# Prompt attention of a hybrid decoder layer: pairs of blocks in alternation, output copied out of PSUM at once, half the copies of the turned weights on VectorE

## The chip, the cores and the metric

The kernel runs on 1 core of one Trainium2 chip. The metric is the device time of one execution in microseconds. A core has TensorE (PE; PEld is its weight load), VectorE (DVE), ScalarE (ACT), GpSimd (POOL) and SyncE (SP), which here starts most of the transfers. The engines run side by side and wait for each other by semaphores only.

## The reference

One inference step of a layer on 1024 prompt tokens and 8 sequences of 4 new tokens, all in float32. Around the attention stand a half-step feed-forward network, a combined input projection, a convolution branch with a LayerNorm and swish, an output mix, and a second feed-forward network. What the change touches is attention over the prompt's selected keys, and the LayerNorm of the convolution branch:

```
s = index_scores(qi, ki, wi); keep the 256 best admissible keys of each query
logits = q . k * HEAD_DIM ** -0.5, NEG where a key is not kept
p = softmax(logits);  out = p @ v            # 8 heads of 64, 8 blocks of 128 queries
y = silu(layernorm(conv(u)));  A = y @ w_conv_out;  B = out @ w_attn_o
h = h + g2 * W_out(sigmoid(gate_A) * A + sigmoid(gate_B) * B)
```

## The kernel before

The prompt's queries are taken in 8 blocks of 128. Block b admits 128 (b + 1) keys, so block 7 has eight times the work of block 0. The selection has left a mask of 0 or NEG in `pick` for each block. Attention is dense over the admitted keys with that mask added. Its loop runs over NQ = 64 heads n in the order of the blocks, block 0 first (b = n // 8), and each engine has its own unrolled copy of the loop, written out in the order in which it is to work:

- TensorE (function `m2_pe`) works in units u of two heads. Iteration u holds the logits of unit u + 1 (L1524, four PSUM banks of `main`, two per head, single), the transposes of the exponentials of head 2u (`turn_weights`, L1541; keys 0 to 511 into bank 4 as part 0, the others into bank 5 as part 1), the values of unit u - 1 (L1552, into bank b % 2 of `aux`, where all 8 heads of a block collect), and the transposes of head 2u + 1. Once in a block the reciprocal sums are turned as well (`turn_sums`, L1563, bank 4).
- VectorE (`m2_dve`) adds the mask and takes the maximum of each head in one operation out of PSUM into `lb` or `lb_raw` (L1785), and makes the bias from it (L1790). For each block it later takes the reciprocal of the sums and spreads it over `otok` (L1803, L1807), multiplies the block's output in PSUM by it (L1813), and makes the low part `o_lo` (L1819).
- ScalarE (`m2_act`) takes the exponential with the sum (L1718, two heads behind VectorE), copies the turned weights of both parts out of PSUM (L1692, `pt` or `pt_n`), copies the turned sums (L1712), and makes the high part `o_hi` (L1724).

The logits of the next unit wait until VectorE has read both heads of the present one (`at_l`). Part 0 of each head waits until ScalarE's last copy has freed bank 4. There is one `otok` for all blocks, so one block's output is finished before the next one's is begun.

In the same loop, at heads 36, 39 and 42 (LN_AT), VectorE does a reciprocal (L1795) and a product (L1798) of the LayerNorm for each third of the tokens; at head 46 ScalarE does its swish (L1699), after which GpSimd splits it into high and low parts (L1394, L1396). The loop's end releases the mix: the first product L244 waits for `mix_free`, which VectorE raises after the last block's L1813, and the attention half of it waits for all of `o_lo`. SyncE loads gates and weights for it after the last transposes (`gate_load`, L1381).

## Time and profile before

| | us |
|---|---|
| median of 3 runs (lowest, highest) | 2939.66 (2937.61, 2944.67) |
| the profiled execution | 2934.1 |
| its span | 2932.3 |
| TensorE busy | 2714.8 (93%) |
| VectorE busy | 1485.8 (51%) |
| GpSimd busy | 925.3 (32%) |
| ScalarE busy | 639.0 (22%) |

Times within the profile are us from the start of the span. A group's line gives the engine, the source line, the operation and its tiles (written <- read) with their shapes. The granted clock is the share of 2.4 GHz that TensorE was allowed: 1.00 is 2.4 GHz, 0.50 is 1.2 GHz. Idle time of an engine that is not the last one costs nothing.

### The profile page before, as it was taken

To read this page: it belongs to the slowest core of one execution; us is meant where nothing else is said; L and a number is where in the kernel's file an instruction comes from. 1 tells how busy PE (TensorE), PEld (TensorE's weight loads), DVE (VectorE), ACT (ScalarE), POOL (GpSimd) and SP (SyncE) were. 2 spreads that over 40 slices of the span, in tenths; PEclk is the share of its full clock that TensorE was granted. 3 is DMA by queue.
4 is the path that set the end of the run, shared out by engine and by line. 5 is a ranking of instruction groups with operands and counts; after the bars stand their busy time and mean duration, and the time that the engine had idled before them with its cause. 6 is when DMAs were issued, how large, how long until landed. Compare 5 with 4: busy or idle time off the path is not lost.

```text
span 2932.3 us, 43345 instructions
## 1 busy us (share of the span) xinstructions
PE 2714.8 (93%) x16036; PEld 2444.0 (83%) x16036; DVE 1485.8 (51%) x2536; ACT 639.0 (22%) x1110; POOL 925.3 (32%) x490
## 2 busy tenths in 40 slices
PE   7999999999998879999998488888989999999998
PEld 3799999999997748788798235588879999999998
DVE  2434444444444548999999846454243333333333
ACT  1411111111111421123344226710041000000113
POOL 0322222222222206634698200122213323233223
PEclk9999999999999889999999689999989999999999
DMA  6322222121222313311122510044101111111111
GB/s 237 120 68 72 72 72 71 65 71 65 72 72 95 88 30 103 89 59 37 58 96 78 207 51 1 1 132 145 44 22 44 49 44 43 50 43 50 43 43 60
DMA packets 207593, 209.68 MB, mean 72 GB/s; under 512 B 13087, under 2 KB 160659, under 8 KB 206601
## 3 DMA queue, kind: packets, MB, share of 16 engines
q1 hardware_dynamic: 197324, 181.56, 19.7%
q10 hardware_dynamic: 10181, 26.90, 2.8%
q8 instruction: 60, 0.98, 0.1%
q14 instruction: 28, 0.23, 0.0%
HBM read 172.89 MB, written 28.94 MB: 69 GB/s over the span
## 4 chain that ended last, share of the span: by engine, by line
PE 68%; DVE 22%; issue 5%; ACT 3%; DVEq 1%; DMA 1%; POOL 0%; SPq 0%; ACTq 0%; POOLq 0%
PE main L244 19%; PE main L246 19%; PE main L245 19%; DVE top L1139 6%; DVE pick L1152 5%; DVE conv_y L1206 3%; PE main L333 1%; DVE pick L1126 1%; PE main L1524 1%; PE main L1541 1%; PE aux L1552 1%; ACT tmp L446 1%; PE aux L414 1%; PE aux L344 1%; PE aux L343 1%
## 5 line engine op out<-in xcount | busy, mean ns | idle before, releaser
L244 PE MATMUL main<-nhi,whi 128*128 128x352 f32 (+1 forms) x3288 | 1077.2, 328 | 28.4 <-DVE nlo L491 16.7
L246 PE MATMUL main<-nhi,wlo 128*128 128x352 f32 (+1 forms) x3288 | 1064.0, 324 | 0.0
L245 PE MATMUL main<-nlo,whi 128*128 128x352 f32 (+1 forms) x3288 | 1064.0, 324 | 0.0
L233 POOL CAST whi<-raw 128x1024 fp32r<-128x1024 f32 x189 | 203.3, 1076 | 1669.2 <-PE main L246 1279.0
L244 PEld LDWEIGHTS main<-nhi,whi 128*128 128x128 f32 (+1 forms) x3288 | 622.8, 189 | 55.9 <-issue 25.3
L245 PEld LDWEIGHTS main<-nlo,whi 128*128 128x128 f32 (+1 forms) x3288 | 624.6, 190 | 1.1
L246 PEld LDWEIGHTS main<-nhi,wlo 128*128 128x128 f32 (+1 forms) x3288 | 622.9, 189 | 1.0
L235 POOL TENSOR_TENSOR wlo<-raw,whi 128x1024 fp32r<-128x1024 f32 x189 | 475.7, 2517 | 15.2
L638 DVE TENSOR_TENSOR tmp<-main,tmp 128x352 f32<-128x352 f32 x132 | 69.2, 525 | 779.8 <-PE main L246 775.6
L657 DVE SCALAR_TENSOR_TENSOR h<-main,ada,h 128x352 f32<-128x352 f32 (+1 forms) x528 | 294.3, 567 | 97.4 <-PE main L246 97.2
L244 PE MATMUL main<-hid_hi,whi 128*128 128x352 f32 x1056 | 342.1, 324 | 0.3
L245 PE MATMUL main<-hid_lo,whi 128*128 128x352 f32 x1056 | 338.6, 321 | 0.0
L246 PE MATMUL main<-hid_hi,wlo 128*128 128x352 f32 x1056 | 338.5, 321 | 0.0
L627 ACT ACTIVATE hid_hi<-tmp 128x352 fp32r<-128x352 f32 x132 | 65.8, 498 | 637.9 <-DVE tmp L638 637.9
L244 PEld LDWEIGHTS main<-hid_hi,whi 128*128 128x128 f32 x1056 | 198.1, 188 | 5.0 <-DVE h L657 3.5
L245 PEld LDWEIGHTS main<-hid_lo,whi 128*128 128x128 f32 x1056 | 198.4, 188 | 0.5
L246 PEld LDWEIGHTS main<-hid_hi,wlo 128*128 128x128 f32 x1056 | 198.0, 188 | 0.0
L625 ACT ACTIVATE tmp<-main 128x352 f32<-128x352 f32 x132 | 60.5, 458 | 550.9 <-PE main L246 550.9
L1139 DVE MAX8 top<-pick 128x8 f32<-128x384 f32 (+5 forms) x192 | 171.4, 893 | 16.5 <-DVEq L1131 0.4
L1152 DVE MATCH_REPLACE8 pick<-top,pick 128x384 f32<-128x384 f32 (+5 forms) x192 | 168.2, 876 | 0.4 <-issue 0.3
L641 DVE TENSOR_TENSOR hid_lo<-tmp,hid_hi 128x352 fp32r<-128x352 f32 x132 | 69.3, 525 | 74.5 <-ACT hid_hi L627 74.5
L1206 DVE SCALAR_TENSOR_TENSOR conv_y<-uext,taps,conv_y 128x1024 f32<-128x1024 f32 x60 | 91.2, 1520 | 11.3 <-DVE conv_y L1206 10.9
(251 smaller groups left out, 2592.3 us busy)
## 6 DMA issues: line engine op xcount, KB each, us to landing
ada_raw<-in_w_ada SPq DMA_DIRECT2D x18, 2048.0 KB, 8.5
raw<-in_w_gate SPq DMA_DIRECT2D x44, 512.0 KB, 3.9
raw<-in_w_up SPq DMA_DIRECT2D x44, 512.0 KB, 3.8
raw<-in_w_down SPq DMA_DIRECT2D x44, 512.0 KB, 3.5
raw<-in_w_in SPq DMA_DIRECT2D x40, 512.0 KB, 3.9
gate_d<-zraw ACTq DMA_DIRECT2D x16, 528.0 KB, 2.8
gates<-gate_d SPq DMA_DIRECT2D x16, 528.0 KB, 4.7
zsw<-zraw ACTq DMA_DIRECT2D x50, 132.0 KB, 2.4
```

The costliest lines, as they stand in the source:

```text
L233: pool.tensor_copy(whi[:, slot], raw[:, slot]).then_inc(hi_done, 1)
L235: pool.tensor_tensor(wlo[:, slot], raw[:, slot], whi[:, slot].bitcast(F32), ALU.subtract)\
L244: pe.matmul(bank, whi[:, slot, w], hi(c), start=(i == 0), stop=False)
L245: pe.matmul(bank, whi[:, slot, w], lo(c), start=False, stop=False)
L246: last = pe.matmul(bank, wlo[:, slot, w], hi(c), start=False, stop=(i == n - 1))
L627: act.activation(hid_hi[:, sub, tcs(t)], tmp[:, 3 + t, :], ACT.Copy).then_inc(f["hid_hi"], 1)
L638: dve.tensor_tensor(tmp[:, 3 + t, :], main[:, 3 + t, 0:TC], tmp[:, t, :], ALU.mult)\
L641: dve.tensor_tensor(hid_lo[:, sub, tcs(t)], tmp[:, 3 + t, :], hid_hi[:, sub, tcs(t)].bitcast(F32), ALU.subtract)\
L657: dve.scalar_tensor_tensor(h[:, c, t * TC:t * TC + n], main[:, d % NBANK, 0:n], gate[:, c, 0:1], h[:, c, t * TC:t * TC + n], ALU.mult, ALU ...
L1139: dve.max(top8[0:n, :], scores).then_inc(tk, 1)
L1152: dve.match_replace(scores, top8[:, :], scores, TAKEN).then_inc(tk, 1)
L1206: dve.scalar_tensor_tensor(y, uext[:, c, bass.ds(k, SEQ)], taps[:, c, bass.ds(k, 1)], y, ALU.mult, ALU.add).then_inc(cv, 1)
```

## The change

The units come in the order of GROUPS: blocks 7 and 0 alternate, one unit (two heads) of each, then 6 and 1, 5 and 2, 4 and 3. A group has 16 heads. HEADS[n] gives block and head of the n-th head, DONE the order in which blocks end (7, 0, 6, 1, 5, 2, 4, 3), and e is a block's place in it. The finishing steps of a group's first block follow at heads end_of(e) + 0, 2, 6, 8, those of its second at + 2, 10, 14, 16, where end_of(e) = 16 (e // 2 + 1).

```diff
+        o_f = place("o_f", [P, 4, TOK], F32, HB + 16896)
-        sums = place("sums", [P, 2, H], F32, UB + 44384)
-        rinv = place("rinv", [P, 2, H], F32, UB + 44448)
+        sums = place("sums", [P, 4, H], F32, UB + 44384)
+        rinv = place("rinv", [P, 4, H], F32, UB + 45920)
...
+        GROUPS = ((7, 0), (6, 1), (5, 2), (4, 3))
+        UNITS = [(b, hp) for g in GROUPS for hp in range(H // 2) for b in g]
+        HEADS = [(b, 2 * hp + s) for b, hp in UNITS for s in range(2)]
+        PARTS = [(n, p) for n in range(NQ) for p in range(1 + (HEADS[n][0] >= 4))]
+        DONE = [b for g in GROUPS for b in g]
+        def end_of(e):
+            return 2 * H * (e // 2 + 1)
+        def same_bank(b):
+            return max([e + 1 for e in range(DONE.index(b)) if DONE[e] % 2 == b % 2], default=0)
...
 m2_pool, m == 3:
+                    for t in range(NTC):
+                        pool.wait_ge(ln_sem["rs"], t + 1)
+                        y = conv_y[:, :, tcs(t)]
+                        pool.tensor_tensor(y, y, rstd_c[t][:, :].unsqueeze(1).to_broadcast([P, 4, TC]), ALU.mult)\
+                            .then_inc(ln_sem["ml"], 1)
...
 m2_pe, turn_weights(n, turned_sums):
+                    pe.wait_ge(pt_e[part], parts_before(i, part))
+                    if part == 0:
+                        pe.wait_ge(o_c, turned_sums)
 m2_pe, values(u):
-                pe.wait_ge(pt_e, LAST_PART[2 * u + 1])
-                if hp == 0 and b >= 2:
-                    pe.wait_ge(at_m, b - 1)
+                pe.wait_ge(pt_e[0], 2 * u + 2)
+                if b >= 4:
+                    pe.wait_ge(pt_e[1], parts_before(LAST_PART[2 * u + 1], 1))
+                if hp == 0:
+                    pe.wait_ge(o_u, same_bank(b))
 m2_pe, the loop:
+                for e in range(NSEQ):
+                    if 2 * u == end_of(e) + 2 + 8 * (e % 2):
+                        turn_sums(e, min(2 * u + 1, NQ - 1))
+                        turned_sums = e + 1
...
 m2_act, turned(n), part 0 only:
+                act.activation(pt_of(n)[:, 0:k1, :], main[:, 4, 0:P * k1].rearrange("p (k n) -> p k n", n=P), ACT.Copy)\
+                    .then_inc(pt_e[0], 1)
...
 m2_dve, turned(n), part 1, called after the softmax of head n + 2:
+                dve.wait_ge(pt_t, i + 1)
+                dve.tensor_copy(pt_of(n)[:, 4:k1, :], main[:, 5, 0:P * (k1 - 4)].rearrange("p (k n) -> p k n", n=P))\
+                    .then_inc(pt_e[1], 1)
 m2_dve, the loop, for each e with b = DONE[e] and at = end_of(e) + 8 * (e % 2):
+                    if n == end_of(e) + 2 * (e % 2):
+                        dve.wait_ge(pv_mm, LAST[b] + 1)
+                        dve.tensor_copy(o_f[:, :, bass.ts(b, P)], aux[:, b % 2, :].rearrange("p (c n) -> p c n", c=4))\
+                            .then_inc(o_u, 1)
+                    if n == at + 2:      # reciprocal and spread, as before
...
+                    if n == at + 6:
+                        dve.wait_ge(o_c, e + 1)
+                        dve.wait_ge(o_u, e + 1)
+                        dve.tensor_tensor(otok[:, :].rearrange("p (c n) -> p c n", c=4), o_f[:, :, bass.ts(b, P)],
+                                          otok[:, :].rearrange("p (c n) -> p c n", c=4), ALU.mult).then_inc(at_m, 1)
+                        if e == NSEQ - 1:
+                            dve.drain().then_inc(mix_free, 3)
+                    if n == at + 8:      # o_lo, as before
```

The output's copy `o_f` lies in the place of `o_hi`. TensorE turns the sums of block e in the iteration of heads end_of(e) + 2 (+ 8), ScalarE copies them at + 5 (+ 8) and makes `o_hi` at + 7 (+ 8).

## Rows read from the trace of the kernel before

**Rows 1.** The page, busy time, share of the span and instructions by engine.
```profile
PE 2714.8 (93%) x16036; PEld 2444.0 (83%) x16036; DVE 1485.8 (51%) x2536; ACT 639.0 (22%) x1110; POOL 925.3 (32%) x490
```

**Rows 2.** By stretch: length; PE, PEld, DVE, ACT, POOL busy; granted clock; DMA.
```profile
1844.09:1876.51 32.42, 23.50 (x195) 16.67 (x195) 11.59 (x28) 25.75 (x50) 13.99 (x6) 0.84 0.00 1
...
1748.85:1910.09 161.24, 132.93 (x1088) 87.07 (x1088) 81.91 (x229) 111.46 (x255) 13.99 (x6) 0.89 0.03 8
...
1750.35:1770.90 20.55, 18.51 (x82) 9.63 (x82) 7.80 (x44) 12.03 (x44) 0.00 (x0) 0.50 0.00 0
...
1849.70:1859.60 9.90, 5.71 (x38) 4.75 (x38) 1.85 (x4) 7.79 (x16) 9.74 (x5) 0.50 0.01 2
```

**Rows 3.** Chain of waits, blocks 3, 4, 7: start, us, what.
```profile
1787.20 1.18 PE main L1524 x4
...
1790.48 1.13 PE main L1524 x4
...
1802.33 1.35 PE main L1524 x8
...
1806.10 1.40 PE main L1524 x8
...
1887.65 1.92 PE main L1524 x8
1889.57 1.02 PE main L1541 x8
1890.59 1.90 PE aux L1552 x32
...
1895.03 1.92 PE main L1524 x8
```

**Rows 4.** Timeline, two softmax heads of block 7 on VectorE.
```profile
1889.60 1.23 DVE L1785 CUSTOM_DVE_ANT_0 lb<-main,pick 128x1024 f32<-128x1024 f32 x1 [2.33 <-PE main L1524]
...
1891.01 1.22 DVE L1785 CUSTOM_DVE_ANT_0 lb<-main,pick 128x1024 f32<-128x1024 f32 x1
```

**Rows 5.** Groups by shape, attention: count, busy us, mean ns, idle before.
```profile
L1692 ACT ACTIVATE pt<-main 128x512 f32<-128x512 f32 x24 | 13.9, 596 | 11.5 <-PE main L1541 11.4
...
L1785 DVE CUSTOM_DVE_ANT_0 lb<-main,pick 128x896 f32<-128x896 f32 x4 | 4.4, 1088 | 3.9 <-PE main L1524 3.9
...
L1718 ACT ACTIVATE lb<-lb,nb 128x896 f32<-128x896 f32 x4 | 4.2, 1042 | 0.0
```

**Rows 6.** Groups by shape, VectorE, 10 to 140 us: copies out of PSUM.
```profile
L323 DVE COPY h<-main 128x512 f32<-128x512 f32 x16 | 10.0, 682 | 3.8 <-PE main L297 3.8
...
L323 DVE COPY h<-main 128x128 f32<-128x128 f32 x2 | 0.5, 277 | 0.0
```

**Rows 7.** Groups by shape, attention: operations of the LayerNorm.
```profile
L1396 POOL TENSOR_TENSOR conv_lo<-conv_y,conv_hi 128x1408 fp32r<-128x1408 f32 x3 | 9.5, 3162 | 0.2
...
L1795 DVE RECIPROCAL rstd_c<-rstd_c 128x352 f32<-128x352 f32 x3 | 7.0, 2342 | 0.0
...
L1798 DVE TENSOR_TENSOR conv_y<-conv_y,rstd_c 128x1408 f32<-128x1408 f32 x3 | 4.9, 1626 | 0.1
```

**Rows 8.** Timeline, swish and what follows it.
```profile
1842.66 1.28 ACT L1699 ACT_TABLE_LOAD   x1
...
1850.94 1.28 ACT L1718 ACT_TABLE_LOAD   x1
...
1853.89 1.51 PE L1541 MATMUL main<-cst,lb_raw 128*128 128x128 f32 x6 [8.03 <-ACT pt L1692]
...
1855.49 0.69 DVE L1819 TENSOR_TENSOR o_lo<-otok,o_hi 128x512 fp32r<-128x512 f32 x1 [8.31 <-ACT o_hi L1724]
```

**Rows 9.** Timeline, end of the stage.
```profile
1905.31 0.81 SPq L1381 DMA_DIRECT2D gates<-gate_d  x2
...
1909.29 0.69 DVE L1813 TENSOR_TENSOR otok<-aux,otok 128x512 f32<-128x512 f32 x1 [4.72 <-ACT otok L1712]
...
1910.09 0.43 PE L244 MATMUL main<-conv_hi,whi 128*128 128x352 f32 x1 [1.46 <-DVEq L1815]
```

More of the change, by code:

```diff
@@ L1515, in logits @@
             def logits(u):
[L1517 removed]
+                b, hp = UNITS[u]
                 if u:
@@ L1534, in turn_weights @@
                         continue
-                    before = [j for j in range(i) if PARTS[j][1] == part]
-                    if before:
-                        pe.wait_ge(pt_e, before[-1] + 1)
-                    if part == 0 and n % H == 4 and n > H:
-                        pe.wait_ge(o_c, n // H)
+                    pe.wait_ge(pt_e[part], parts_before(i, part))
+                    if part == 0:
+                        pe.wait_ge(o_c, turned_sums)
                     for k in range(4 * part, min(4 * part + 4, b + 1)):
@@ L1566, in m2_pe @@
             logits(0)
-            for u in range(NQ // 2 + 2):
+            turned_sums = 0
+            for u in range(NQ // 2 + 7):
                 if u + 1 < NQ // 2:
@@ L1702, in ln_swish @@
                 last.then_inc(ln_sem["af"], 1)
-            for n in range(NQ + 8):
+            for n in range(NQ + 17):
                 if 2 <= n < NQ + 2:
@@ L1776, in m2_dve, with turned @@
             dve.wait_ge(v_out, 16 * 9)
-            for n in range(NQ + 10):
+            def turned(n):
+                if (n, 1) not in PARTS:
+                    return
+                i = PARTS.index((n, 1))
+                if n >= 4:
+                    dve.wait_ge(pv_mm, n - 3)
+                dve.wait_ge(pt_t, i + 1)
+                k1 = HEADS[n][0] + 1
+                dve.tensor_copy(pt_of(n)[:, 4:k1, :], main[:, 5, 0:P * (k1 - 4)].rearrange("p (k n) -> p k n", n=P))\
+                    .then_inc(pt_e[1], 1)
+            for n in range(NQ + 17):
                 if n < NQ:
-                    b = n // H
+                    b = HEADS[n][0]
                     w = P * (b + 1)
@@ L1795, in m2_dve @@
                     dve.reciprocal(rstd_c[t][:, :], rstd_c[t][:, :]).then_inc(ln_sem["rs"], 1)
-                    dve.wait_ge(ln_sem["rs"], t + 1)
-                    y = conv_y[:, :, tcs(t)]
-                    dve.tensor_tensor(y, y, rstd_c[t][:, :].unsqueeze(1).to_broadcast([P, 4, TC]), ALU.mult)\
-                        .then_inc(ln_sem["ml"], 1)
-                if n % H == 2 and n > H:
-                    b = n // H - 1
-                    dve.wait_ge(at_e, H * (b + 1))
-                    dve.reciprocal(rinv[:, b % 2, :], sums[:, b % 2, :]).then_inc(at_r, 1)
-                    dve.wait_ge(at_r, b + 1)
-                    if b:
-                        dve.wait_ge(o_l, b)
-                    dve.tensor_copy(otok[:, :].rearrange("p (h d) -> p h d", h=H),
-                                    rinv[:, b % 2, :].unsqueeze(2).to_broadcast([P, H, HD])).then_inc(at_o, 1)
@@ L1809, in m2_dve @@
-                if n % H == 6 and n > H:
-                    b = n // H - 1
-                    dve.wait_ge(o_c, b + 1)
-                    dve.wait_ge(pv_mm, H * (b + 1))
-                    dve.tensor_tensor(otok[:, :], aux[:, b % 2, :], otok[:, :], ALU.mult).then_inc(at_m, 1)
-                    if b == 7:
-                        dve.drain().then_inc(mix_free, 3)
-                if n % H == 0 and n > H:
-                    b = n // H - 2
-                    dve.wait_ge(o_h, b + 1)
-                    dve.tensor_tensor(o_lo[:, :, bass.ts(b, P)], otok[:, :].rearrange("p (c n) -> p c n", c=4),
-                                      o_hi[:, :, bass.ts(b, P)].bitcast(F32), ALU.subtract).then_inc(o_l, 1)
+                for e in range(NSEQ):
+                    b, at = DONE[e], end_of(e) + 8 * (e % 2)
+                    if n == end_of(e) + 2 * (e % 2):
[3 more added lines that the diff above has]
+                    if n == at + 2:
+                        dve.wait_ge(at_e, LAST[b] + 1)
+                        dve.reciprocal(rinv[:, e % 4, :], sums[:, e % 4, :]).then_inc(at_r, 1)
+                        dve.wait_ge(at_r, e + 1)
+                        if e:
+                            dve.wait_ge(o_l, e)
+                        dve.tensor_copy(otok[:, :].rearrange("p (h d) -> p h d", h=H),
+                                        rinv[:, e % 4, :].unsqueeze(2).to_broadcast([P, H, HD])).then_inc(at_o, 1)
+                    if n == at + 6:
[6 more added lines that the diff above has]
+                    if n == at + 8:
+                        dve.wait_ge(o_h, e + 1)
+                        dve.tensor_tensor(o_lo[:, :, bass.ts(b, P)], otok[:, :].rearrange("p (c n) -> p c n", c=4),
+                                          o_hi[:, :, bass.ts(b, P)].bitcast(F32), ALU.subtract).then_inc(o_l, 1)
```

69 lines of the change are left out of this document (34 added, 35 removed).

## The prediction

> **What bounds the kernel now.** I read the page first, then the busy time by stretch, the chain of waits over the prompt attention, the groups by shape, and the timeline at the ends. The page shows TensorE busy for 93% of the span [rows 1]: the large products before and after attention are TensorE's own, and the change touches none of them. What it touches is one stage, the loop over 64 heads of prompt attention, from the first logits at 1748.85 to the first mix product at 1910.09: 161.24 us, 5.5% of the span, in which TensorE is busy for 132.93 us, ScalarE 111.46, VectorE 81.91 [rows 2]. Of TensorE's time much is at half clock: from 1750.35 to 1770.90 (granted clock 0.50, the 1.2 GHz level, with the light blocks 0 and 1 running) and from 1849.70 to 1859.60 (0.50 again, after a hole) [rows 2]. Taking half of the busy time of these two and of a short third one near 1834 (18.51, 5.71 and about 3.5 us busy) off, TensorE has 132.9 - 13.9 = 119 us of work at 2.4 GHz, of which eight turnings of sums are 0.63 each. So some 42 us of the stage are holes or half clock. The stretch from block 6's first logits to block 7's, with the swish in it, takes 32.42 us for 23.50 of TensorE [rows 2]. Where nothing special comes between, the units run at TensorE's pace: 5.86 us for two heads of block 7 (logits 1.92, transposes twice 1.02, values 1.90), and from one logits to the next 3.77 at block 4 and 3.28 at block 3 [rows 3].
>
> **The change: order of the units.** A unit is two heads. The same 32 units are run, so TensorE's work stays. A heavy unit A and a light B now alternate. The logits of all four banks are single: the logits of B may start only when VectorE has read both heads of A, and between them TensorE has only B's transposes, A's values and B's transposes. I follow one A, B period of blocks 7 and 0 at full clock from the start of A's logits. VectorE can begin 1.95 to 2.0 us after it (logits 1887.65, softmax 1889.60), and one head takes it 1.41 from start to start (1889.60 to 1891.01; the 1.22 operation and its two small ones); exp of the first head starts at about 3.5 [rows 4]. Exp takes 1.04 for 896 columns, so about 1.15 for 1024, and 1.2 with its read; B's small copy 0.3, partly beside; exp of the second head 1.2; the copy of the first head's part 0 0.60; wait 0.12; transposes of A's second head 1.03 [rows 3 to 5]. That ends at 7.9 and only then come A's next logits. TensorE's own work in it is 5.86 + about 1.3 = 7.2. For blocks 6 and 1 the same chain with 1.09 for VectorE and 1.04 for exp gives 7.4 against TensorE's 7.15; for 5 and 2 TensorE's own 7.2, for 4 and 3 its 7.3 (3.77 plus 0.22 for one block more in the values, and 3.28; block 5 and 2 interpolated from these and block 6, about 0.6 per block) [rows 3, 5]. Four pairs of each: 4 x (7.9 + 7.4 + 7.2 + 7.3) = 119.2. TensorE alone would be about 115. The alternation by itself therefore gives nothing: the heavy blocks were TensorE's already, and their chain is now longer by 4.
>
> **Half the copies on VectorE.** The second part (blocks 4 to 7) leaves ScalarE: 32 copies, 0.60 us at 512 columns and about half of it at 128; ScalarE was not last in steady running. On VectorE a copy out of PSUM was 0.682 for 512 columns and 0.277 for 128 [rows 6]; it stands between the softmax of B's first and second head, waits there for A's transposes, and in the periods above it fits (TensorE waits neither for it nor for B's second head; 0.4 to 0.5 us remain). Queued behind it are B's second softmax and through that A's next logits. Cost 0 with that cover; without it up to 32 x 0.5 = 16 us. I take 0, the nearest end as VectorE is busy some 5 of 7.9 us. That VectorE keeps its order shows at 1855.49: it had stood 8.31 us for ScalarE's o_hi, with its next head's softmax behind [rows 8].
>
> **Sums, output and o_f.** Per block VectorE now has four insertions: the new copy out of PSUM (0.68 by [rows 6]), reciprocal and spread (about a copy's time, 0.63), the product 0.69 [rows 9], o_lo 0.69 [rows 8]. Six blocks' insertions fall into groups 1 to 3. At an A place (o_lo; the new copy of the first block) they delay the second head of A, for whose end the logits of B wait with 0 to 0.45 us to spare: 0.65, 0.65, 1.25, 0.55, 0.9, 0.25 = 4.2. At a B place (the others, two coming together at each group's third head) the spare is 0.4 to 0.55: about 1.6 + 1.4 + 1.9 = 4.8. I take 9.0. Ends: 0, as o_lo cost next to nothing at block 3, whose iterations stayed at 3.28 [rows 3], and all of it, 6 x (0.68 + 0.63 + 0.69 + 0.69) = 16.
> The turning of the sums stands in PE's queue behind a copy that now waits for exp of A: transposes 0.63, then ScalarE's copy 0.60 before A's second exp. Following it through the period: +1.4 each (block 7's iteration with it, 1887.65 to 1895.03, was 7.38 against 5.86: +1.5) [rows 3]. Six inside: 8.4 (ends 0.63 x 6 = 3.8 and 1.7 x 6 = 10.2).
> The product used to read PSUM, 0.69 for 512 columns, and the copy costs what it costs; its gain is a bank free earlier. The first values of a block now wait for the copy of the last block in the same bank; for block 6 that is block 0's, placed after VectorE's third head of the group, while these values stand behind another logits and transposes of 1.5 us or more: 0, or a few tenths four times without that cover.
>
> The Trainium skill (VectorE: DVE Perf Modes, § Rules for kernel authors) would copy a matmul's output out of PSUM first only where many operations follow; here one follows. By that rule the copies are a pure cost of 8 x 0.68 = 5.5 us of VectorE; the sum above has them in its 9.0 where they are not covered.
>
> **LayerNorm.** Three products of 1.63 leave VectorE for GpSimd (nearest row there: 3.16 for a two-input operation of the same 128x1408 shape, 9.5 for three) and have until head 46; cover is two units, 7 us, for the last, 0 cost; if it weren't, the wait is at most 9.5. VectorE's three reciprocals of 2.34 stay: at an A place +2.3, at a B1 place +1.0, at a B place together with an insertion +2.6: 6 [rows 7] (ends 4 and 7). Before, 3 x (2.34 + 1.63) = 11.9 stood there. ScalarE's swish stays: 1842.66 to the end of the second table load at 1852.22 is 9.6; TensorE stood 8.03 us and then ran at half clock until 1859.60 [rows 2, 8]. Now at exp of a light head with 1.0 to 1.8 spare: hole 8.6, then half clock 2.5: 11.1 (ends 8 and 14).
>
> **Start.** Block 7 comes first: logits 1.92, softmax 1.41, table load 1.28, exp 1.2 twice, copy, transposes: the first logits of the second A start at about 9.3 instead of 7.9: +1.4. The clock will fall in the hole after the first logits (it fell at 1750.35, in block 0's first units). Ends for the half clock: 0, and half of the 18.51 us that TensorE was busy at it, 9.3. After the swish, on dense block 6, it lasted 5.7 us from the first transposes to 1859.60, and here too dense work follows, so I take 7 us of it, 3.5 lost.
>
> **End.** Before, the last values ended at 1908.04; sums 0.63, ScalarE 0.60, product 0.69, mix at 1910.09: 2.05 [rows 9]. Now the groups end with blocks 4 and 3, whose sums use one tile otok in turn: from where another logits would have started, 0.7 of ScalarE's copy, transposes 0.6, values of 4 1.24, transposes 0.6, copy and waits 0.85, values of 3 1.0 = 5.0 to the end of the last values (light blocks' lengths from [rows 3] and [rows 5], scaled), then sums(4) 0.6, copy 0.65, product 0.75, o_hi 0.65, o_lo 0.75, reciprocal and spread 0.7, sums(3) 0.7, copy 0.6, product 0.75, mix 0.1: 6.4. Together 11.4 (ends: 9, and 14 if the clock falls there). SyncE's loads of gates and weights for the mix, issued from 1905.31 on at the last transposes [rows 9], get 5 us more and stay hidden.
>
> **Sum.** 119.2 + 9.0 + 8.4 + 6 + 11.1 + 1.4 + 3.5 + 11.4 = 170.0 against 161.2: +8.8. The profiled execution was 2934.1 us, its span 2932.3, so a like one would take 2942.9; it lay 5.6 below the median of the runs shown, 2939.66. With +8.8, rounded up for the chance that the clock also falls at the end: **2949 us**.
>
> **Rivals.**
> (1) The balance works. TensorE is the only bound, since each heavy unit's softmax is covered by the light one: the periods fall to TensorE's 115 (-4.2) and VectorE's insertions cost nothing (-9), as at block 3. Then 170.0 - 13.2 = 156.8, -4.4: 2935. It decides at the point where TensorE's work between A's logits and B's (2.4 us at full clock for 7 and 0) outlasts VectorE's two heads (2.7: 0.05 + 1.41 + 1.25). For it: VectorE is busy only half of the stage, ScalarE's load falls. Against: the two heads are just longer. With the start kept at 2.4 GHz (-3.5) and half of LayerNorm hidden (-3) as well it gives -11: 2929, clearly faster.
> (2) The clock. The half clock lasts 20.5 us at the start as before, now on the heaviest blocks (+6.5), and falls at the end (+2.5): 2958. For it: TensorE was busy 18.51 of 20.55 us there and the clock stayed low [rows 2]. Against: after the swish it came back in 5.7 us.
> (3) The insertions are half hidden and the end costs 2 less: 2943, no change to be told.
> (4) It doesn't do what it says: the bank is freed early, but nothing waited for it; that is inside the sum and has no price of its own. If GpSimd's products were late for the swish, +3 to +9: 2952 to 2958.
>
> **Chances.** Own forecast 0.42; (1) without its extras 0.16, with them 0.12; (2) 0.13; (3) 0.12; (4) late 0.05. A difference of 0.3% (8.8 us) is about what can be told from none: slower by over it 0.45 (0.27 of my own case, whose value lies just past that bound, and (2) and (4)), within 0.42 (the rest of my own, (1) bare, (3)), faster 0.13. The likeliest case's own range is 2943 to 2955; for 8 of 10 it has to reach (1) and (2): 2932 to 2959.
>
> **What would show it.** In the profile after: logits of a light unit starting when VectorE's second heavy head ends (wait of logits on the softmax, 0.2 to 1.3 us each); periods of 7.9 with blocks 7 and 0 and near 7.3 with 4 and 3; some 11 us from the last softmax to the first mix product; TensorE idle 8 us at the swish; in the stage VectorE busy about 97 us (81.9 + 15 of copies of 0.28 to 0.68 + 5.5 - 4.9) and ScalarE about 96 (111.5 less 16 of second parts). It is wrong if the stage lasts under 162 us: first if the insertions cause no waits of TensorE, next if the clock doesn't fall at the start.

## The result, and the profile after

The changed kernel takes 2950.96 us (median of 7, 2946.46 to 2954.99); the kernel before, in 7 executions beside it, 2939.34 (2937.61 to 2944.67). That is 11.6 us more, a ratio of 1.004 (95% interval 1.0028 to 1.0051): slower by a little more than 0.3%. The forecast was 2949, its range 2932 to 2959. The profiled execution of the kernel after took 2952.8, its span 2951.0.

The page after, busy time by engine, against [rows 1]:

```profile
PE 2722.4 (92%) x16036; PEld 2448.2 (83%) x16036; DVE 1510.3 (51%) x2573; ACT 630.2 (21%) x1078; POOL 936.5 (32%) x493
```

TensorE has the same 16036 instructions. VectorE has 37 more (32 copies of second parts, 8 copies out of PSUM, 3 products fewer), ScalarE 32 fewer, GpSimd 3 more. Next the busy time by stretch of the kernel after, to be laid beside [rows 2]: the four groups of blocks (7 and 0, 6 and 1, 5 and 2, 4 and 3 up to its last heavy logits), the end, the whole stage from the first logits to the first mix product, and one spell of half clock. The columns are length, busy PE, PEld, DVE, ACT, POOL, granted clock, DMA share, GB/s:

```profile
1753.55:1787.93 34.38, 29.30 (x227) 19.21 (x227) 19.07 (x55) 19.21 (x45) 0.00 (x0) 0.90 0.00 1
1787.93:1823.21 35.28, 30.26 (x272) 19.96 (x271) 22.56 (x65) 22.14 (x52) 0.00 (x0) 1.00 0.00 1
1823.21:1870.60 47.39, 35.48 (x271) 23.22 (x271) 33.85 (x70) 23.72 (x51) 9.50 (x3) 0.86 0.00 1
1870.60:1907.09 36.49, 25.82 (x200) 16.79 (x201) 17.29 (x52) 26.67 (x55) 13.91 (x6) 0.81 0.00 1
1907.09:1926.87 19.78, 12.67 (x124) 8.83 (x123) 10.34 (x27) 10.80 (x23) 0.00 (x0) 0.99 0.37 119
1753.55:1926.87 173.32, 133.53 (x1089) 88.00 (x1089) 103.11 (x266) 102.54 (x223) 23.41 (x9) 0.90 0.05 14
1759.60:1766.00 6.40, 6.17 (x22) 4.18 (x24) 1.74 (x5) 3.26 (x10) 0.00 (x0) 0.50 0.00 0
```

The stage lasts 173.32 us against 161.24. The third group stands out: 47.39 us where the second, with nearly the same work of TensorE, takes 35.28. The remaining difference between the two profiled executions, 18.7 less 12.1, lies outside the stage: the first logits come 4.7 us later (1753.55 for 1748.85), in a part that the change doesn't touch, and about 2 us follow the stage. The early start is the kernel before's: E2, E3 and E12 below, which change nothing ahead of the stage either, start at 1754.55, 1751.83 and 1751.47. That profiled execution, 2934.1, was 5.2 under its kernel's median.

One period of blocks 7 and 0 in the chain of waits of the kernel after (start, us, what), which answers to [rows 3] and [rows 4]:

```profile
1772.58 1.97 PE main L1547 x8
1774.54 1.21 DVE lb L1819
...
1775.96 1.21 DVE lb L1819
1777.16 0.02 DVE mx L1819
...
1777.23 0.49 PE main L1547 x4
1777.72 1.02 PE main L1562 x8
1778.74 0.37 PE aux L1575 x4
...
1779.22 1.07 PE main L1562 x8
1780.29 0.62 PE main L1547
```

The reader is to see one hand-over: the light unit's logits at 1777.23 start as soon as VectorE has read the second heavy head (1777.18). TensorE stood only 0.32 us for it. From 1772.58 to 1780.29 the period is 7.71. ScalarE is not in this chain: heavy logits, VectorE's two heads, light logits and TensorE's own work follow each other.

The swish, from the timeline of the kernel after (start, us, engine, line, operation, tiles; in brackets the idle time before it and what ended that), against [rows 8]:

```profile
1869.43 1.28 ACT L1720 ACT_TABLE_LOAD   x1
1870.73 6.96 ACT L1720 ACTIVATE conv_y<-conv_y,par 128x352 f32<-128x352 f32 x12
1877.71 1.28 ACT L1741 ACT_TABLE_LOAD   x1
...
1880.29 0.87 PE L1562 MATMUL main<-cst,lb_raw 128*128 128x128 f32 x3 [8.35 <-ACT lb_raw L1741]
```

And the end in the chain of waits, against [rows 9]:

```profile
1919.68 1.09 PE aux L1575 x16
1920.78 0.60 PE main L1586 x4
...
1923.42 0.69 DVE o_lo L1855
...
1924.26 0.44 DVE otok L1844
...
1924.74 0.67 PE main L1586 x4
...
1926.07 0.69 DVE otok L1849
...
1926.87 0.66 PE main L244
```

From the end of the last values (1920.77) to the mix at 1926.87 it is 6.1 us, where the kernel before had 2.05: two blocks' sums go through the one tile otok one after the other.

### The profile page after: what moved, and what is told of

It reads as the page before. It is cut to its first block, busy times and chain, and to the rows that moved or that the text cites. A ratio compares the mean times of both kernels' runs of the same rounds, so it can differ in the third digit from the quotient of the medians.

```text
span 2951.0 us, 43396 instructions
## 1 busy us (share of the span) xinstructions
PE 2722.4 (92%) x16036; PEld 2448.2 (83%) x16036; DVE 1510.3 (51%) x2573; ACT 630.2 (21%) x1078; POOL 936.5 (32%) x493
## 4 chain that ended last, share of the span: by engine, by line
PE 67%; DVE 22%; issue 5%; ACT 3%; DVEq 1%; DMA 1%; POOL 0%; SPq 0%; ACTq 0%; POOLq 0%
PE main L244 19%; PE main L246 19%; PE main L245 19%; DVE top L1139 6%; DVE pick L1152 5%; DVE conv_y L1206 3%; DVE pick L1126 1%; PE main L333 1%; PE main L1547 1%; PE main L1562 1%; ACT tmp L446 1%; PE aux L414 1%; PE aux L344 1%; PE aux L343 1%; PE aux L342 1%
## 5 line engine op out<-in xcount | busy, mean ns | idle before, releaser
L1206 DVE SCALAR_TENSOR_TENSOR conv_y<-uext,taps,conv_y 128x1024 f32<-128x1024 f32 x60 | 91.2, 1520 | 11.3 <-DVE conv_y L1206 10.9
```

Source lines behind the costliest of these rows:

```text
L1206: dve.scalar_tensor_tensor(y, uext[:, c, bass.ds(k, SEQ)], taps[:, c, bass.ds(k, 1)], y, ALU.mult, ALU.add).then_inc(cv, 1)
```

## The experiments

Each kernel's median is compared with that of the kernel before in executions on the same chip (2938.85 to 2940.05). "Stage" is the profiled execution's. The stage is that of one execution, and spells of half clock fall differently in it: the first group, which is the same work in the kernel after, E1, E7 and E15, took 34.38, 35.88, 35.25 and 32.83. So the verdicts go by the medians, and the stage says where to look. One of the ten executions of E2 lies far out, at 6136.58; without it the median is 2939.68.

| | kernel | stage | median (n) | less before | ratio (95%) |
|---|---|---|---|---|---|
| | before | 161.2 | 2939.34 (7) | | |
| | after | 173.3 | 2950.96 (7) | +11.6 | 1.0040 (1.0028-1.0051) |
| E1 | after, LayerNorm's products on VectorE | 174.1 | 2953.44 (4) | +13.4 | 1.0047 (1.0029-1.0064) |
| E2 | before, products on GpSimd | 163.6 | 2940.01 (10) | 0.0 | 1.0000 (0.9990-1.0010) |
| E3 | before, second parts' copies on VectorE | 165.6 | 2945.22 (10) | +5.2 | 1.0022 (1.0011-1.0033) |
| E4 | after, blocks 0 to 7 one after the other | 170.9 | 2951.38 (5) | +11.3 | 1.0041 (1.0026-1.0055) |
| E12 | before, with the copy out of PSUM alone | 175.5 | 2953.70 (4) | +14.9 | 1.0047 (1.0030-1.0064) |
| E13 | order and copy out alone | 166.6 | 2947.20 (10) | +8.3 | 1.0031 (1.0021-1.0040) |
| E8 | before, LayerNorm ahead of attention | 142.3 | 2923.72 (4) | -15.1 | 0.9941 (0.9925-0.9958) |
| E7 | after, LayerNorm ahead | 149.4 | 2931.69 (10) | -8.1 | 0.9974 (0.9965-0.9984) |
| E9 | E8 with the copies on VectorE | 142.7 | 2923.02 (5) | -15.9 | 0.9949 (0.9936-0.9963) |
| E5 | after, 100 idle transposes at the swish, bank 4 | 185.0 | 2961.73 (4) | +22.9 | 1.0071 (1.0055-1.0088) |
| E15 | the same in bank 5 | 170.6 | 2953.05 (4) | +13.3 | 1.0047 (1.0030-1.0065) |
| E14 | E8 with idle transposes at the start | 144.4 | 2925.57 (5) | -14.2 | 0.9954 (0.9938-0.9969) |

**E1 and E2: where the LayerNorm's products run.** E1 takes the three products off GpSimd in the kernel after; E2 puts them there in the kernel before.

```
-                        pool.wait_ge(ln_sem["rs"], t + 1)
-                        y = conv_y[:, :, tcs(t)]
-                        pool.tensor_tensor(y, y, rstd_c[t]..., ALU.mult).then_inc(ln_sem["ml"], 1)
...
+                    dve.wait_ge(ln_sem["rs"], t + 1)
+                    dve.tensor_tensor(y, y, rstd_c[t]..., ALU.mult).then_inc(ln_sem["ml"], 1)
```

> The kernel after with the three products back on VectorE. Theory (GpSimd's products hold VectorE up): o_lo and spread all at 0.69 and 0.43 us, and the 4.9 us of products on VectorE in their place, so stage 171 to 176, no change to after that can be told. Rival (moving them was a gain): stage 177 or more.

> The kernel before with only the three LayerNorm products moved to GpSimd. Theory (while GpSimd works on two inputs, a VectorE operation with two inputs in SBUF or a copy within SBUF stands until it ends, as o_lo 2.87 and the spread 3.41 us in the profile after): the 4.9 us taken off VectorE come back as one long spread (over 2 us more) and one long o_lo; stage 159 to 164. Rival (the move is a gain): every VectorE operation keeps its length, stage 155 to 158.

Both theories came in: stages of 174.1 (171 to 176) and 163.6 (159 to 164). E2 costs nothing and gains nothing (0.0); E1 lies 1.8 above the kernel after, less than the intervals can tell. Five microseconds of VectorE's work left it and brought nothing. The timelines say why. First the kernel after, VectorE and GpSimd in the third group:

```profile
1844.47 0.90 DVE L1819 CUSTOM_DVE_ANT_0 lb<-main,pick 128x768 f32<-128x768 f32 x1
...
1845.47 2.87 DVE L1855 TENSOR_TENSOR o_lo<-otok,o_hi 128x512 fp32r<-128x512 f32 x1
...
1855.28 3.41 DVE L1844 COPY otok<-rinv 128x512 f32<-128x512 f32 x1
...
1844.63 3.17 POOL L1413 TENSOR_TENSOR conv_y<-conv_y,rstd_c 128x1408 f32<-128x1408 f32 x1 [3.90 <-DVE rstd_c L1831]
1855.27 3.15 POOL L1413 TENSOR_TENSOR conv_y<-conv_y,rstd_c 128x1408 f32<-128x1408 f32 x1 [7.47 <-DVE rstd_c L1831]
```

The o_lo operation, 0.69 us elsewhere ([rows 8], and the end above), started 0.84 us behind a GpSimd product and lasted 2.87, until 0.54 us after the product's end. The spread of the reciprocals (a copy from SBUF to SBUF), 0.43 to 0.44 elsewhere, started with the next product and lasted 3.41, until 0.27 us after its end. The softmax operation at 1844.47, which reads PSUM, ran its 0.90 beside the same product undisturbed. The kernel of E2, which has neither the new order nor the new copies, shows the same two in its timeline:

```profile
1825.57 2.88 DVE L1820 TENSOR_TENSOR o_lo<-otok,o_hi 128x512 fp32r<-128x512 f32 x1
...
1835.85 3.42 DVE L1808 COPY otok<-rinv 128x512 f32<-128x512 f32 x1
```

With the products on VectorE (E1) the groups by shape show the two kinds back at their length but for one of seven (807 ns is a mean), and the products' own 4.9 us:

```profile
L1854 DVE TENSOR_TENSOR o_lo<-otok,o_hi 128x512 fp32r<-128x512 f32 x7 | 5.6, 807 | 10.5 <-ACT o_hi L1742 10.5
...
L1829 DVE TENSOR_TENSOR conv_y<-conv_y,rstd_c 128x1408 f32<-128x1408 f32 x3 | 4.9, 1625 | 0.1
L1843 DVE COPY otok<-rinv 128x512 f32<-128x512 f32 x8 | 3.4, 427 | 0.3
```

In the kernel after the same two groups are 7.8 and 6.4 us, together 5.2 more, for the 4.9 that left. The products' work moved, their time on VectorE stayed.

**E3, E12, E13 and E4: copies, copy out of PSUM, and order.** E3 is the kernel before with the second parts' copies on VectorE:

```
-                for i, (m, part) in enumerate(PARTS):
...
+            def turned(n):
+                if (n, 1) not in PARTS:
+                    return
...
+                dve.tensor_copy(pt_of(n)[:, 4:k1, :], main[:, 5, 0:P * (k1 - 4)]...).then_inc(pt_e[1], 1)
...
+                if 2 <= n < NQ + 2:
+                    turned(n - 2)
```

> The kernel before with one part of the change: the second part's copies (blocks 4 to 7) on VectorE, order of the blocks as before. Theory (order is what costs): the copies are covered, the attention stage (161.2 us before, 173.3 after) stays at 159 to 163 and the time within 0.1% of before. Rival (VectorE's queue is what costs: the copy waits for transposes with the next softmax behind it): stage 165 or more, the time 4 us or more longer.

It costs 5.2 us, where the prediction had 0, as the rival wanted (165.6); but its reason, the queue, is only a small part of it in the trace. The stage's extra 4.4 us lie in blocks 4 and 5; what the others gain and lose cancels. By stretch, from block 4's first logits to block 6's, E3 and then the kernel before:

```profile
1802.65:1852.81 50.16, 40.18 (x318) 27.23 (x317) 35.00 (x76) 26.51 (x52) 0.00 (x0) 0.86 0.00 1
```

```profile
1798.53:1844.09 45.56, 35.82 (x317) 24.61 (x317) 31.40 (x63) 28.87 (x65) 0.00 (x0) 0.96 0.00 1
```

Of the 4.6 us, 4.4 are TensorE busy longer with the same work, at a mean granted clock of 0.86 instead of 0.96. In these stretches its logits waited for VectorE's softmax 7.0 us in E3 and 7.9 before; a wait of 1.6 for a copy is new. E12 is the kernel before with nothing but the copy of a finished block out of PSUM, at the third head of the next block:

```
-                    pe.wait_ge(at_m, b - 1)
+                    pe.wait_ge(o_u, b - 1)
...
+                    dve.wait_ge(pv_mm, H * (b + 1))
+                    dve.tensor_copy(o_f[:, :, bass.ts(b, P)], aux[:, b % 2, :]...).then_inc(o_u, 1)
...
-                    dve.tensor_tensor(otok[:, :], aux[:, b % 2, :], otok[:, :], ALU.mult).then_inc(at_m, 1)
+                    dve.tensor_tensor(otok..., o_f[:, :, bass.ts(b, P)], otok..., ALU.mult).then_inc(at_m, 1)
```

> The kernel before with only the copy of each block's output out of PSUM into o_f at the block's third following head; order, copies of the weights and LayerNorm as before. The run with all edits but the order had a stage of 170.9 us; copies on VectorE alone 165.6 (+4.4), products on GpSimd alone 163.6 (+2.3). Theory (the parts add up): this part is the remaining +3: stage 163 to 166. Rival (it is covered by VectorE's idle time): 160 to 162, and then the parts hurt only together.

It costs 14.9 us for 8 copies of 0.69: neither the theory (163 to 166) nor the rival (160 to 162) comes near its 175.5. Its timeline at block 2's third head:

```profile
1783.09 0.69 DVE L1805 COPY o_f<-aux 128x512 f32<-128x512 f32 x1 [1.17 <-PE aux L1554]
...
1784.27 0.55 DVE L1787 CUSTOM_DVE_ANT_0 lb_raw<-main,pick 128x384 f32<-128x384 f32 x1
...
1784.88 0.59 PE L1526 MATMUL main<-ka,qa 64*128 64x384 f32 x2 [1.28 <-DVE mx L1787]
```

VectorE stands 1.17 us for the last values of the block, with the next head's softmax queued behind the copy; then come copy, reciprocal and spread, and TensorE stands 1.28 us for that softmax before the next logits (0.16 at the same place before). In the whole stage VectorE waited 9.7 us for last values, in 7 waits, and the logits waited 17.3 us for softmax, where it was 10.1 before. This is what the copy's place in the queue costs. By the profile's list of waits, the kernel before and E12 (waiting line, what it waited for, us in total, times, longest):

```profile
PE main L1524 <- DVE mx L1785: 10.1, 9, 3.8
```

```profile
PE main L1526 <- DVE mx L1787: 17.3, 13, 4.3
```

It is not all of the 14.9. TensorE is busy for 138.97 us in this stage and for 132.93 in that of the kernel before, with the same work: the granted clock is 0.85 against 0.89, and the half clock at the start lasts until about 1782, 30 us and not 20. Where both have a clock of 1.00, in block 3, E12 takes 15.89 us and the kernel before 14.64: 1.25 for one copy of 0.69. Whether the copies bring the longer half clock about no run separated. E13 has the copy out and the alternation, with the second parts' copies back on ScalarE and the products back on VectorE:

```
-            def turned(n):
...
+                if (n, 1) in PARTS:
+                    act.wait_ge(pt_t, PARTS.index((n, 1)) + 1)
...
+                    act.activation(pt_of(n)[:, 4:k1, :], main[:, 5, 0:P * (k1 - 4)]..., ACT.Copy).then_inc(pt_e[1], 1)
```

> The kernel after with the second part's copies back on ScalarE and the products back on VectorE: what is left of the change is the alternation with the copy out of PSUM that it needs. Theory of the prediction (the alternation makes the chain of a pair longer by itself and its end is longer): stage 170 to 176, with the second copies in ScalarE's chain of the heavy unit rather more than after's 173.3. Rival (the order costs only the 2.4 us between 170.9 and 173.3, the rest is the copies): stage 164 to 168.

It costs 8.3; the stage, 166.6, is the rival's (164 to 168). So with the copy out in place the alternation gives 14.85 - 8.35 = 6.5 us back (the intervals of the two ratios just overlap, the executions hardly do: 2951.71 and more, and 2951.76 and less). VectorE waits less for last values, 4.2 us for 9.7, but the logits wait as long for softmax, 16.7 us for 17.3; in the traces the gap is TensorE's busy time, 128.87 for 138.97, at a clock of 0.93 for 0.85. The stretch of E13 that answers to the third group of the kernel after (a steady period of blocks 7 and 0 is 7.74 in E13, 7.71 in the kernel after):

```profile
1818.01:1861.55 43.54, 33.11 (x271) 21.30 (x270) 30.52 (x64) 25.68 (x59) 0.00 (x0) 0.92 0.01 1
```

From E13 to E1 only the copies differ, and they cost 13.39 - 8.35 = 5.0 again (here the two intervals overlap, so by itself this isn't clear of noise). The third group is 47.69 in E1, 4.15 more:

```profile
1823.82:1871.51 47.69, 36.05 (x270) 23.77 (x271) 33.71 (x73) 23.72 (x51) 0.00 (x0) 0.86 0.00 0
```

This is the group in which the LayerNorm's reciprocals stand. Of the 4.15, 2.9 are TensorE busy for longer at the lower clock (0.86 for 0.92). E4 undoes the order alone:

```
-        GROUPS = ((7, 0), (6, 1), (5, 2), (4, 3))
+        GROUPS = ((0,), (1,), (2,), (3,), (4,), (5,), (6,), (7,))
```

> The kernel after with its blocks one at a time, 0 first, as before; the copy out of PSUM, the copies on VectorE and the products on GpSimd stay. Theory (the alternation and its end cost the 12 us): stage 160 to 166, the time back to within 0.2% of before. Rival (the copy out of PSUM and the other edits cost): stage 169 or more.

It is as slow as the kernel after (+11.3 and +11.6), and its stage, 170.9, is the rival's. So the 6.5 that the alternation gives back between E12 and E13 are not to be had once the other edits are in. E4, with the copies on VectorE besides, lies 3.5 below E12. Laid side by side, the stages show where such differences sit (busy time and granted clock by stretch, wait of the logits by the list of waits):

| | stage | TensorE busy | granted clock | logits waited for softmax |
|---|---|---|---|---|
| before | 161.2 | 132.93 | 0.89 | 10.1 |
| E2, products on GpSimd | 163.6 | 136.84 | 0.86 | 8.3 |
| E3, copies on VectorE | 165.6 | 137.97 | 0.87 | 9.2 |
| E12, copy out | 175.5 | 138.97 | 0.85 | 17.3 |
| E4, all but the order | 170.9 | 134.25 | 0.89 | 18.4 |
| after | 173.3 | 133.53 | 0.90 | 18.7 |
| E1, after, products on VectorE | 174.1 | 134.50 | 0.89 | 18.6 |
| E13, order and copy out | 166.6 | 128.87 | 0.93 | 16.7 |
| E8, LayerNorm ahead | 142.3 | 129.98 | 0.92 | 2.1 |
| E9, E8 with copies on VectorE | 142.7 | 129.87 | 0.92 | 3.5 |
| E7, after, LayerNorm ahead | 149.4 | 125.79 | 0.96 | 11.3 |

With the LayerNorm in the loop, the logits wait 8.3 to 10.1 us for softmax without the copy out of PSUM, and 16.7 to 18.7 with it, in either order; with the LayerNorm ahead it is 2.1 and 3.5 without, 11.3 with it. That is the part of the cost which the runs show cleanly. The work of TensorE is the same in all, so where its busy time differs the clock was another: from E12 to E4 it falls by 4.7 and the stage by 4.6, from E12 to E13 by 10.1 and the stage by 8.9.

**E8, E7 and E9: the LayerNorm out of the loop.** The third sum of squares follows the first two, and reciprocals, products and swish are done before the first head:

```
+            for t in range(NTC):
+                ln_swish(t)
...
-                if n == LN_AT + 10:
-                    for t in range(NTC):
-                        ln_swish(t)
...
-                if n in range(LN_AT, LN_AT + 9, 3):
-                    t = (n - LN_AT) // 3
-                    dve.wait_ge(ln_sem["sd"], t + 1)
-                    dve.reciprocal(rstd_c[t][:, :], rstd_c[t][:, :]).then_inc(ln_sem["rs"], 1)
```

> The kernel before with the LayerNorm taken out of the attention loop: the third sum of squares on TensorE right behind the first two, reciprocals and products on VectorE in its idle 20 us before the attention, swish on ScalarE there too, GpSimd's splits right after. Theory (LayerNorm and swish are 18 to 20 us of holes and half clock in the stage, hidden work before it): stage 141 to 146, the start of it later by at most 3; time 2920 to 2925, ratio 0.993 to 0.995. Rival (the holes come back elsewhere, as the half clock at the start of the stage lasts as long as there are light blocks): stage 150 or more.

> The kernel after with the LayerNorm ahead of the attention, as in the version of the kernel before that took 142.3 us. What is left of the change's cost is then the order, the copy out of PSUM, the copies on VectorE and the longer end. Theory (6.6 us of the 12 were GpSimd's products, the reciprocals beside insertions, and the half clock that followed): the loss against that version shrinks from 12 to 4 to 8 us: stage 146 to 150. Rival (the copies on VectorE and the insertions cost by themselves): stage 153 or more.

> The version of the kernel before with the LayerNorm ahead of the attention (stage 142.3 us) with the second part's copies on VectorE besides. Copies on VectorE cost 5 us in either order as long as LayerNorm's reciprocals stood in VectorE's loop, though the steady periods kept their length. Theory (it was the reciprocals and what followed them, copy and softmax queued behind): without them the copies cost nothing, stage 141 to 144, the time as without them, ratio 0.993 to 0.996. Rival (the copies cost by themselves, each block's special events included): stage 146 or more, ratio 0.996 or more.

On the kernel before it gains 15.1 us and gives, with E9, the fastest kernel of all; all three theories hold by stage and time. Only the first logits of E8 come 7.3 us later than before, where at most 3 was expected. The busy time by stretch of E8, the 31 us ahead of the stage and the stage:

```profile
1725.00:1756.12 31.12, 29.64 (x84) 9.74 (x83) 15.44 (x9) 12.70 (x19) 10.15 (x4) 1.00 0.06 17
1756.12:1898.41 142.29, 129.98 (x1089) 84.58 (x1089) 70.45 (x223) 101.72 (x241) 5.33 (x3) 0.92 0.03 10
```

Ahead of attention TensorE is busy for 29.64 of 31.12 us at full clock, and the LayerNorm runs beside it on engines that had nothing to do. The stage shrinks by 19. The changed kernel gains as well (E7), but stays 7.0 above E8. The third and the fourth group of E7, to be laid beside the 47.39 and 36.49 of the kernel after:

```profile
1826.38:1860.56 34.18, 30.17 (x271) 19.87 (x271) 22.17 (x67) 23.18 (x53) 0.00 (x0) 1.00 0.00 1
1860.56:1885.49 24.93, 22.21 (x201) 14.63 (x201) 16.31 (x52) 17.70 (x39) 0.00 (x0) 1.00 0.01 1
```

The LayerNorm cost the third group 13.2 us and the swish the fourth 11.6. E9 moves the copies to VectorE on top of E8: -15.9 against -15.1, no cost any more. In E8 and E9 the clock stays at 1.00 over blocks 4 and 5. So the 5 us of the copies arise only with the LayerNorm in the loop, and not in the steady periods; whether by VectorE's queue or by the half clock that falls there, E9 doesn't tell, since it takes both away.

**E5, E15 and E14: the price of half clock.** E5: idle transposes keep TensorE busy in the hole of the swish:

```
+                if n == LN_AT + 10:
+                    pe.wait_ge(pt_e[0], n)
+                    for _ in range(100):
+                        pe.transpose(main[:, 4, 0:P], ident, ident)
```

> The kernel after with 100 extra transposes of the identity into bank 4 in TensorE's hole of the swish (head 46), which nothing reads. Theory (the half clock after the hole costs 2 to 5 us): the granted clock stays 1.00 behind it and the stage is 169 to 171. Rival (the hole itself is the cost and the half clock is covered by ScalarE's backlog): stage 172 to 174.

> The kernel after with 100 extra transposes, as tried before, but into bank 5, which is free in the hole of the swish; the earlier try stood behind ScalarE's copy out of bank 4 and so behind the hole. Theory (half clock after the hole costs 2 to 5 us): granted clock 1.00 behind the swish and stage 168 to 171. Rival: stage 172 or more.

E5 failed as an experiment, with a stage of 185.0. The timeline of its TensorE:

```profile
1884.19 11.03 PE L1557 MATMUL main<-cst 128*128 128x128 f32 x76 [8.31 <-ACT pt L1718]
```

The fillers waited for bank 4, which ScalarE's copy frees only after the swish. They didn't fill the 8.31 us of the hole, they followed it, 11 us long (76 of the 100 are in the record): +11.3 on the kernel after. In E15 they go to bank 5 and run in the hole:

```profile
1870.56 11.13 PE L1557 MATMUL main<-cst 128*128 128x128 f32 x100
1881.53 0.49 PE L1566 MATMUL main<-cst,lb_raw 128*128 128x128 f32 x3
```

The clock stays at 1.00 behind them, but at 0.11 us each they outlast the hole (from the logits' end to the unit's transposes it is now 10.9 us, against 8.35), and the median is no better (+13.3). Its stage, 170.6, is the theory's, and the trace holds the price of the half clock there: from the transposes behind the swish to the last heavy logits it takes 23.59 us (1881.53 to 1905.12), and 26.80 in the kernel after (1880.29 to 1907.09): 3.2 us. That the median shows nothing of it stays unexplained; in the profiled execution 2.7 us more follow the stage than in that of the kernel after. E14 does the same at the start of E8, 36 transposes before the first head and 4 before each of the next 15:

```
+                if n < 2 * H:
+                    for _ in range(36 if n == 0 else 4):
+                        pe.transpose(main[:, 5, 0:P], ident, ident)
```

> The version with the LayerNorm ahead of the attention (stage 142.3 us, the first 20 us of it at half clock) with extra transposes of the identity that nothing reads: 36 before the first head's and 4 before each of the next 15 heads', into a bank that blocks 0 to 3 don't use. Theory (the fall at the start comes from TensorE's hole behind the first logits, and costs 5 to 9 us): granted clock 1.00 or falling later than 1752, stage 134 to 139. Rival (light blocks' short instructions bring the half clock in any case, and the extra ones lie on the path): stage 142 to 146.

Its busy time by stretch, from the third unit's logits to block 2's first, and the stage; then the first of these in E8:

```profile
1763.06:1779.35 16.29, 15.66 (x128) 10.84 (x127) 7.46 (x39) 9.76 (x38) 0.00 (x0) 1.00 0.00 1
1753.78:1898.14 144.36, 133.49 (x1185) 92.97 (x1185) 70.49 (x223) 101.55 (x241) 5.35 (x3) 0.98 0.03 10
```

```profile
1760.53:1779.12 18.59, 17.96 (x79) 9.21 (x79) 7.45 (x39) 9.79 (x37) 1.00 (x1) 0.50 0.00 0
```

From about 1760 on the granted clock is 1.00 where the kernel before had 0.50, and over the stage 0.98 instead of E8's 0.92; the stage is 2 us longer, not shorter, as the rival wanted (142 to 146), and the gain on the kernel before 0.9 smaller (14.2 for 15.1, no difference that can be told). A unit of block 0 takes 2.18 us from logits to logits there (1763.06 to 1765.24) and 2.17 in E8 at half clock (1762.70 to 1764.87). Block 1's four units do gain, 11.93 us (1767.42 to 1779.35) for 14.25 (1764.87 to 1779.12), fillers included. So the clock gave 2.3 us back over these light blocks, and more than that was spent ahead of them: the first two units, with the first 40 fillers, take 9.28 us (1753.78 to 1763.06) for 4.41 in E8 (1756.12 to 1760.53). What is shown is that as the fillers stand nothing was left over, not that half clock is free here.

## Why the prediction was right, and where only its total was

The time came out 1.96 us above the forecast and inside the range; the sign and the size of the case held. Step by step:

- **Steady periods: right, slightly too long.** Predicted 7.9 for blocks 7 and 0, measured 7.71, with the light logits released by VectorE's second heavy head as described (waits 0.3 us, predicted 0.2 to 1.3). The path was another than mine: I had added up ScalarE's two exponentials and its copy before the last transposes, but the chain shown above goes through VectorE's two heads and TensorE's own work (7.3 of the 7.71). The second group took 35.28; the terms for it (4 x 7.4 = 29.6, its insertions and sums 5.7) give 35.3. None of its periods is free of insertions, so only the sum is tested. In the recorded sum the parts of the insertions add up to 9.15, not 9.0, and those of the end's second half to 6.25, not 6.4; the two slips cancel.
- **"The alternation by itself gives nothing": the size right, the meaning not.** With all edits in, it holds (E4 and the kernel after are equal). But the copy out of PSUM, which I priced within 9.0 of insertions, costs 14.9 alone in the old order (E12) and 8.3 together with the new one (E13). The order isn't a cost of 4 on top of the copies; while the copies of the turned weights are ScalarE's it takes 6.5 off the cost of the copy out. What I had not counted is VectorE's wait for the last values (9.7 us in E12, 3.5 in the kernel after), with a softmax behind it; the logits' wait for softmax rose from 10.1 to 17.3 and 18.7.
- **"I take 0" for the copies on VectorE: the step that failed.** They cost 5.2 (E3) and 5.0 (E13 to E1). The cover that I named, 0.4 to 0.5 us of slack in a steady period, is there: periods are 7.71 with and 7.74 without. The cost appears in the stretch of the LayerNorm, where a reciprocal of 2.34 stands in the same queue, and there for the most part as TensorE's work at half clock (4.4 of 4.6 us in E3), a term that I didn't have in that place at all; with the LayerNorm elsewhere the cost is gone (E9). The bound of 16 that I kept for lost cover was the right thing to keep.
- **LayerNorm 6: mis-sized, measured 13.2.** The third group took 47.39 where its terms (4 x 7.2, insertions and sums 6, LayerNorm 6) made 40.8; without the LayerNorm it takes 34.18 (E7), near the other terms' 34.8. Three things are in the 6.6. Half clock: I had none in this group, but the granted clock was 0.50 in two spells of some 6 us each from 1848 on, and TensorE's busy time was 35.48 for E7's 30.17 at 1.00. The products on GpSimd, "0 cost", held VectorE's operations with two SBUF inputs and the SBUF copy until they ended: 5.2 us of VectorE in the place of 4.9. And the copies of the point before fall into this group, 4.15 of it in E1. The three overlap, so they don't add up. That E1 and the kernel after have the same group (47.69 and 47.39) shows that the move was neutral here, not harmful. The trace of the kernel before had shown the hold, in its convolution, where I didn't look. Its timeline there, VectorE and GpSimd:

```profile
1605.16 3.08 DVE L1206 SCALAR_TENSOR_TENSOR conv_y<-uext,taps,conv_y 128x1024 f32<-128x1024 f32 x1 [0.20 <-DVE conv_y L1206]
...
1604.05 3.11 POOL L1245 TENSOR_TENSOR conv_y<-conv_y,zsw 128x1024 f32<-128x1024 f32 x1 [0.17 <-POOL conv_y L1245]
```

  And the durations of that line, shortest, median and longest in ns:

```profile
L1206 DVE SCALAR_TENSOR_TENSOR conv_y<-uext,taps,conv_y x60: 1283/1284/3108, 1601.9 to 1707.2; 128x1024 f32<-128x1024 f32 x60
```

  The same operation on the same shape takes 1.28 or 3.1 us, and 3.1 is found beside GpSimd's two-input operation. The Trainium skill (SBUF — State Buffer, § SBUF: two separate sides) says that VectorE and GpSimd share a pair of ports as "an exclusive lock, not a bandwidth split", held for a whole instruction, and that it catches VectorE's operations with two SBUF inputs against a GpSimd operation that reads SBUF, and its fast fp32 copies. By that rule, which I had not weighed, both long operations are expected; the trace agrees (2.87 for 0.69, 3.41 for 0.43, and 0.90 for the softmax from PSUM unchanged).
- **Busy times.** VectorE in the stage 103.1 (predicted 97; the hold is 5.2 of the 6.1), ScalarE 102.5 (predicted 96; the 32 copies are 13.0 us, not 16, and some had overlapped other work, so that the busy time fell by 8.9).
- **Start and half clock: near.** The first group took 34.38, the terms (31.6, 1.4, 3.5) make 36.5. The spell at the start was 6.4 us long, predicted 7, not the 20.5 that the second rival wanted. Its price was set at half of the busy time. In E14 the clock gave 2.3 us back over the light blocks, fillers included, where half of the busy time would be 9; for the heavy start no run measured it.
- **Swish and end: near.** From group 4's first heavy logits to its last 36.49 (terms 38.9), and 24.93 without the swish (E7): 11.6 for it, forecast 11.1; the half clock in it 3.2 by E15, forecast 2.5. The end 19.78 from the last heavy logits (7.3 + 11.4 = 18.7), of it 6.1 behind the last values (6.4).
- **The rivals.** The balance (1) would need VectorE's two heads to end before TensorE's work between the logits: TensorE had done its part and stood 0.32 us for them. It fell, by little. That the freed bank gives nothing (4) holds: in the kernel before the values never waited for it (their one wait in the loop, 0.8 us, was for ScalarE's copy), and in the kernel after they don't either.

The stage was forecast at 170.0 and took 173.3: the third group 6.6 over its terms, the end 1.1 over, the first group 2.1 and the fourth 2.4 under. The total came within 2 us partly because errors of both signs met, and that is luck: the third group alone was 6.6 off.

What stays open: why the copies on VectorE cost 5 us in both orders. E3, E1 and E9 tell the place, not the instruction; most of it shows as half clock, and in that cause and consequence weren't separated. The same holds for the 6 us of TensorE's busy time in E12's cost. No run held the clock at 1.00 over the LayerNorm's stretch with the LayerNorm in place. Nor did a run take the two-block end apart; its 4 us are read from the chain. E7 less E8, 7.0, says what order, copy out, copies and end cost together once the LayerNorm is away; that the end is the larger part of it is only argued.

## What to carry to other kernels

An operation put in an engine's order costs what is queued behind it while it waits, not its duration: 8 copies of 0.69 us cost 14.9 us in one place and order, about half of it (7.2) as logits waiting longer for a softmax behind them, and 32 more cost 5 or nothing, with the LayerNorm in the loop or ahead of it. When two versions of a stage are compared, lay TensorE's busy time beside its waits: the same work at another clock makes up some of the difference, 6 of E12's 14 us and 4.4 of the 4.6 in E3's blocks 4 and 5, and no wait will explain that part. Before work is moved from VectorE to GpSimd, look for the same forms side by side in the trace already there, and compare their shortest and longest durations. In a loop bound by a chain through all engines, first look for what needn't be in it at all: moving the LayerNorm and its two table loads ahead of the loop, under a stretch where TensorE was busy for 95%, gained 15.1 us, more than the whole change lost.

## What the runs showed of the hardware

VectorE's operations don't merely slow down beside a two-input GpSimd operation: o_lo lasted from 1845.47 until 0.54 us behind the end of the product, at 2.87 us for 0.69, and the SBUF copy at 3.41 for 0.43, while a softmax operation reading PSUM kept its 0.90. Half clock (0.50 granted) over the light blocks cost no more than the fillers that kept the clock at 1.00 did: 142.29 us with it, 144.36 with them. What it costs depends on what bounds the unit: a unit of block 0 took 2.17 us at 0.50 and 2.18 at 1.00, block 1's four units 14.25 and 11.93. A 128x128 fp32 transpose took 0.11 us in a row of 100 at full clock (11.13).
